# Two split orders and the doubled key columns in the last layer of a three-layer network

## The chip, the cores and the metric

One Trainium2 chip, one core of it. The metric is the device time of one execution in microseconds (us); lower is better. TensorE does the matrix products, VectorE and ScalarE the elementwise work, GpSimd and SyncE mostly start transfers.

## The reference, cut to what matters

The input is one sequence of 256 rows of 2048 columns in float32. Three layers follow each other: a convolution mixer with an MLP, a pooling mixer with an MLP, and a last layer with three kinds of attention. The change touches the last layer only, between its first products and its heads:

```python
h = rmsnorm_2(x, norm_g) @ w_in                    # 256 x 5388, split into 15 parts
c_q, c_kv, k_rope, ..., q_nsa, k_c, v_c, k_s, ...  # c_q, c_kv: 512 columns; k_c: 192; v_c: 128
q  = rmsnorm_2(c_q,  q_norm_g)  @ w_uq             # ranks -> 8 query heads
kv = rmsnorm_2(c_kv, kv_norm_g) @ w_ukv            # ranks -> 8 key and value heads
# compress: overlapping blocks of 32 rows, one every 16 rows (15 blocks)
k_cmp = silu((blocks(k_c) + pe_k).reshape(15, 32 * 192) @ w1k) @ w2k
v_cmp = silu((blocks(v_c) + pe_v).reshape(15, 32 * 128) @ w1v) @ w2v
```

The norm of `x` has one factor per row (r1). The kernel multiplies by it after the product, when it takes the result out of PSUM.

## The kernel before, in words

**Weights.** All weights run through one ring of four tiles (128 x 2048 numbers, 1 MB, smaller for some) in an order, the plan, that is fixed at build time. `Sync.load_tile` (line 950) starts the load of tile k into place k mod 4 when the products of tile k - 4 are done. Each float32 weight tile is split in two parts for the products: ScalarE writes the rounded part (`Act.split`, line 477, tile `hi`), and VectorE subtracts it from the tile and leaves the rest (`Dve.split`, line 590, tile `raw_r`, the "low" part). TensorE then does three products per block of 128 rows: high by high, high by low, low by high (lines 341). The compress weights `w_ck` and `w_cv` are used whole and are not split (`WHOLE`).

**The order of the work.** All engines run the same Python function `conduct`, and each keeps the instructions that are its own, so the order in which `conduct` calls things is the order of every engine's queue; waits are semaphores. `take(name)` hands out the next tile j and then calls `split_ahead(j + 3)`, which queues the splits of all tiles below that number whose load is already queued. `release(j, done, hold)` calls `load_ahead(j + 5)`, and unless `hold` is set it also calls `split_ahead(j + 4)`. So the split of tile j + 3 is queued when tile j is released, or, with `hold`, at the `take` of tile j + 1. Loads are queued by `release` in both cases.

**Small work between products.** `gemm` (line 1102) takes a tile, does its 24 products and calls `step()` in the middle of a tile and after its `release`. A step runs the next entry of the list `later`, and if that is empty the next of the list `extra`. `fill` runs an entry of `extra` alone.

**The stage around the change.** The products run in this order: `w_i2` (four tiles, 396 columns: k_rope, k_c, v_c and the gates), `w_i0` (four tiles, c_q), one compress piece of `w_ck`, `w_i1` (four tiles, c_kv, with a `w_ck` piece ahead of its last tile), then the heads: two tiles of `w_uq` with a `w_ck` piece between them, and so on. In the numbers of the plan: w_i2 is 332 to 335, w_i0 is 336 to 339, w_ck is 340, w_i1 is 341, 342, 343 and 345 with w_ck 344 between them, w_uq is 346 and 348 with w_ck 347 between, and 349.

- After `w_i2`, `evac` (line 1202) copies both 128-row halves from the PSUM banks to the staging tiles EV with the factor r1 (ScalarE, line 473). ScalarE makes the gates (tanh, line 540), VectorE finishes them, rotates the 64 k_rope columns of both halves (`rope`) and doubles them, and then `tail_rows` (VectorE, line 799) copies the last 64 of the 192 k_c columns twice, side by side, from EV to a tile of 128 columns for each half (`kc_t`, in R_s).
- `kc_turn` (line 1887) turns the first 128 k_c columns and these doubled 64 with four TensorE transposes (line 344). It is the second entry of `later`, so it stands in TensorE's queue right behind the products of tile 336.
- `ranked` (line 1830) is called for c_q (`w_i0`) and for c_kv (`w_i1`). After the products it takes the sum of squares of both halves out of PSUM (ScalarE, line 503), copies both halves to EV (ScalarE, line 473), computes the inverse root with VectorE and GpSimd (lines 582, 933, 574, 577) and multiplies EV by it (VectorE, line 582). The turns of the result are put into `later` behind three `fill` entries: the first two pairs stand behind the second tile of the next products.
- `compress_k` and `compress_v` (lines 1932 and 1942) each take one compress tile, do 8 or 16 small products and release it.

Of the kernel before, what the change touches and what calls it, by code (L numbers as in the profile page):

```python
# [153 lines left out]
def v3(ap, k):  # L154
    return ap.rearrange("p (k n) -> p k n", k=k)
# [142 lines left out]
class Engine:  # L298
# [26 lines left out]
    def idle(self, *a, **k):  # L325
# [7 lines left out]
        product = norm_mean = norm_root = relu_square = residual = rope = rope_keys = scale = scaled_parts = scores = side_load = side_taps = sine = \  # L333
# [233 lines left out]
        self.copy(xs, xs, done, scale=r)  # L567


class Dve(Engine):  # L570


# [218 lines left out]
    def group_sums(self, ready, done):  # L791

        self.wait_ge(ready)
        self.e.tensor_reduce(self.m.group_rows, self.m.group_of, AX.X, ALU.add).then_inc(*self.inc("dve_done", done))

    def tail_rows(self, t, src, ready, done):

        self.wait_ge(ready)
        self.cp(v3(self.m.kc_t[t], 2), src.unsqueeze(1).to_broadcast([128, 2, 64]), done)

    def tail_keys(self, b, ready, done):

# [176 lines left out]
def conduct(E, plan, listing):  # L979
# [3 lines left out]
    m, a, P, EV = E.m, E.a, E.m.P, E.m.EV  # L983
    serial = [0]

    def mark(what):
        serial[0] += 1
        return what, serial[0]
# [5 lines left out]
    def load_ahead(n):  # L994
        while at_["load"] < min(len(plan), n) and not listing:
            k = at_["load"]
            if k >= NS and k - NS not in freed:
                return
            name, i, parts, c = plan[k]
            E.load_tile(k, m.raw[k % NS][0:parts, 0:c], a[name][i], freed.get(k - NS))  # L1000
            at_["load"] += 1
# [36 lines left out]
    def release(j, done, hold=False):  # L1038
        freed[j] = done
        load_ahead(j + 1 + NS)  # L1040
        if not hold:
            split_ahead(j + 2 + AHEAD)


    bank_free, bank_held = [[] for _ in range(8)], set()
# [3 lines left out]
    def pair():  # L1049
        nxt["pair"] ^= 2  # L1050
        return [nxt["pair"], nxt["pair"] + 1]
# [41 lines left out]
    def flush():  # L1093
        while later:
            later.pop(0)()
# [6 lines left out]
    def gemm(name, xh, xl, x_names, nk, c, k0=0, steps=1, hold=False, lead=False, tail=False, late=False):  # L1102
        banks = pair()
        n = nk // 4
        groups = [[q] for q in range(n)]
        if lead:
            groups[0:2] = [[0, 1]]
        if tail:
            groups[-2:] = [[n - 2, n - 1]]
        done = [None, None]  # L1110

        def product(q, j, wh, wl, k, t):
            kk = k0 + 4 * q + k
            while x_names[kk] is None or (isinstance(x_names[kk], list) and x_names[kk][t] is None):
                step()
            x_ready = x_names[kk][t] if isinstance(x_names[kk], list) else x_names[kk]
            h, l = (x[kk][:, 128 * t:128 * t + 128] if isinstance(x, list) else x[:, kk, 128 * t:128 * t + 128] for x in (xh, xl))
            done[t] = ("product", j, t)
            E.product(P[banks[t]][:, 0:c], h, l, wh[:, k, :], wl[:, k, :], j, k, q == 0 and k == 0, q == n - 1 and k == 3,
                      x_ready, bank_free[banks[t]], done[t])  # L1120

        for group in groups:
            blocks = []
            for q in group:
                at_["pause"] = at_["pause"] or late and q == n - 1
                j, wh, wl = take(name)
                blocks.append((q, j, v3(wh, 4), v3(wl, 4)))
            turns = [(0, 1)] if len(group) == 1 else [(0,), (1,)]
            for ts in turns:
                for q, j, wh, wl in blocks:  # L1130
                    for k in range(4):
                        for t in ts:
                            product(q, j, wh, wl, k, t)
                        if k == 1 and steps > 1:
                            step(steps - 1)
                    if ts[-1] == 1:
                        release(j, done[1], hold and q == n - 1)
                    if steps:
                        step()
        return banks, done if tail else done[1]  # L1140
# [61 lines left out]
    def evac(banks, ready, c=512, scale=m.R1, scale_m=None):  # L1202
        ks, ms = [], []
        for t in range(2):
            k, done = ev(hold=True), mark("evacuated")
            E.copy_out(EV[k][:, 0:c], P[banks[t]][:, 0:c], [ready, scale_m], ev_free[k], done, scale=scale[:, t:t + 1])
            bank_free[banks[t]] = [done]
            ks.append(k)
            ms.append(done)
        return ks, ms  # L1210
# [12 lines left out]
    def side_load(sem, o, i, *free):  # L1223
        done = mark("side load")
        E.side_load(sem, o, i, list(free), done)
        return done
# [134 lines left out]
    XT, HH, HL, MH, ML, M, GA = m.XT, m.HH, m.HL, m.MH, m.ML, m.M, m.GA  # L1361
# [39 lines left out]
    h_m, r1_m, sq_m = [None] * 16, [], []  # L1401
# [188 lines left out]
    for n, kind in enumerate(kinds):  # L1590
        banks, done = gemm("w_z", HH, HL, h_m, 16, 512, steps=2)
# [3 lines left out]
        ks, ms = evac(banks, done, scale_m=list(r1_m))  # L1595
# [14 lines left out]
    for g in range(4):  # L1610
        banks, done = gemm("w_mo", MH, ML, mix_m, 16, 512, steps=3 if g == 0 else 1, hold=g == 3, tail=g == 3, late=g == 3)
# [141 lines left out]
    banks, done = gemm("w_mkv", HH, HL, memory["x"], 16, 512, steps=2, hold=True)  # L1753
    scale_m = load_row(2, 0, x_m[3])
    row_m = load_row(3, 1, x_m[3])
    ks, ms = evac(banks, done, scale=m.R4, scale_m=memory["r"])
# [18 lines left out]
    for c in range(0, 16, 2):  # L1775
        b, done = bank(), mark("windows")
# [6 lines left out]
    d_done = done  # L1783
# [7 lines left out]
    for g in range(4):  # L1791
        banks, done = gemm("w_p", MH, ML, d_m, 4, 512, k0=4 * g)
# [33 lines left out]
    h_m, r1_m, x_m = x_columns(x_get, HH, HL, GA[4])  # L1826
# [1 line left out]
    rope_m = side_load("c9", m.st[:, 32:160], a["c_rope"], memory["r"])  # L1828

    def ranked(name, th, tl, gain):  # L1830
        banks, done = gemm(name, HH, HL, h_m, 16, 512, steps=2)
        flush()
        sm = [square_sum(P[banks[t]][:, :], m.SUMC[:, t, :], [done, list(r1_m)], scale=m.R1[:, t:t + 1]) for t in range(2)]
        ks, ms = evac(banks, done, scale_m=list(r1_m))
        r = rstd(m.SUMC, 512, m.R3, sm)
        ns = [mark("ranked"), mark("ranked")]
        for t, k in enumerate(ks):
            E.scale(EV[k][:, :], EV[k][:, :], m.R3[:, t:t + 1], [r, ms[t]], ns[t])
        names, parts = columns(lambda t, c: EV[ks[t]][:, 128 * c:128 * c + 128], [ns], 4, th, tl, gain)

        def run(i):
            turned = both_of(parts[i])
            if i == 1:
                for k in ks:
                    let_go(k, turned)
        later.extend([fill, fill, fill, lambda: run(0), lambda: run(1)])
        return names
# [10 lines left out]
    banks, done = gemm("w_i2", HH, HL, h_m, 16, 396, steps=2, lead=True)  # L1858
    flush()
    ks, ms = evac(banks, done, 396, scale_m=list(r1_m))  # L1860
    side_load("c13", m.PEK, a["pe_k"], *x_m)
    side_load("c13", m.PEV, a["pe_v"])
    side_load("c13", m.C2K, a["w_c2k"])
# [12 lines left out]
    def kpe_turn():  # L1876
# [2 lines left out]
        E.rope_keys(b, done, list(gain_free), copied)  # L1879
        bank_free[b] = [copied]  # L1880
        kpe_m.extend([copied, done])

    kt = [mark("k tail"), mark("k tail")]
    for t in range(2):
        E.tail_rows(t, EV[ks[t]][:, 192:256], [ms[t], d_done], kt[t])

    def kc_turn():
        b, done, copied = bank(), mark("turn"), mark("copied")
# [43 lines left out]
    def compress_k(q):  # L1932
        if q == 0:
            cmp_m["b"] = bank(hold=True)
        b = cmp_m["b"]
        j, w = take("w_ck")
        rows = [8 * q + r for r in range(8)]
        E.compress(P[b][:, 0:192], [m.BK[:, l, :] for l in rows], [blk_m["a", q // 2] if q < 4 else blk_m["b", q - 4]] * 8,
                   v3(w, 8), q == 0, q == 5, j, bank_free[b], ("product", j, 1))
        release(j, ("product", j, 1))  # L1940

    def compress_v(q):
        b = cmp_m["b"]
        j, w = take("w_cv")
        rows = [16 * q + r for r in range(16)]
        E.compress(P[b][:, 192:320], [m.BV[:, l, :] for l in rows], [blk_m["v", l // 16] for l in rows],
                   v3(w, 16), q == 0, q == 1, j, None, ("product", j, 1))
        release(j, ("product", j, 1))
        cmp_m["done"] = ("product", j, 1)

    later += [nop, kc_turn, vc_turn, blocks_a, blocks_b, blocks_v, kpe_turn]
# [73 lines left out]
    banks, done = gemm("w_uq", m.CQH, m.CQL, cq_m, 4, 512, steps=2)  # L2025
# [15 lines left out]
    for g in range(2):  # L2041
        banks, ranks_done = gemm("w_ukv", m.CKH, m.CKL, ck_m, 4, 512, steps=2)
# [10 lines left out]
    banks, done = gemm("w_i3", HH, HL, h_m, 16, 512, steps=2)  # L2053
# [159 lines left out]
    banks, done = gemm("w_i4", HH, HL, h_m, 16, 512, steps=2)  # L2213
# [7 lines left out]
    banks, done = gemm("w_i5", HH, HL, h_m, 16, 384, steps=2)  # L2221
# [6 lines left out]
    banks, done = gemm("w_i6", HH, HL, h_m, 16, 512, steps=2)  # L2228
# [45 lines left out]
    for g in range(4):  # L2274
        banks, done = gemm("w_o2", oh, ol, o_cols, 16, 512, steps=2 if g == 0 else 1, tail=g == 3)
        for t in range(2):
# [4 lines left out]
            if g == 3:  # L2281
                r = rstd(m.SUMA, D, m.R2, [sums[2 * q + t] for q in range(4)], t)
# [87 lines left out]
```

## Time and profile before

| | us |
|---|---|
| median of three runs | 2367.03 |
| lowest and highest of them | 2365.26, 2368.86 |
| the profiled execution, its own time | 2365.16 |
| its span in the profile | 2363.4 |
| TensorE busy | 2336.7 (99%) |
| VectorE busy | 1303.4 (55%) |
| ScalarE busy | 1080.9 (46%) |

The span runs from the first to the last instruction; the other 1.8 us of the execution's time lie around it. TensorE is busy nearly all the time at a granted clock of 0.999 of full speed, so a change can win only what is left of its idle time, or lose by adding to it. The times at the start of rows below are counted from the start of the span.

### The profile page before, as it was taken

What the parts mean: (1) busy time and instruction counts of PE and PEld (TensorE: products, weight loads), DVE (VectorE), ACT (ScalarE), POOL (GpSimd) and SP (SyncE); (2) the same over time, 40 slices, a digit from 0 to 9 for tenths busy, and PEclk for the clock granted to TensorE, in tenths of its full rate; (3) what the DMA queues carried; (4) which work ended last, traced back from release to release, by engine and by line L of the source; (5) the groups of instructions that cost most, each with busy time, mean ns of one, the idle gap of its engine ahead of it and who ended that gap; (6) DMA issues with size and microseconds to landing.
All of it is one profiled execution on the core that took longest, in us unless ns stands there. A gap on an engine that the chain in (4) does not pass through costs nothing.

```text
span 2363.4 us, 25257 instructions
## 1 busy us (share of the span) xinstructions
PE 2336.7 (99%) x10937; PEld 1933.5 (82%) x10937; DVE 1303.4 (55%) x1325; ACT 1080.9 (46%) x1164; POOL 27.0 (1%) x46
## 2 busy tenths in 40 slices
PE   8999999999999999999999999999999999999998
PEld 6778788888888888888888888888888888888887
DVE  5665855544554554556764454554544584556654
ACT  6444444644344344354565444344344364344443
POOL 0000000000000000000000000000000010000000
PEclk9999999999999999999999999999999999999999
DMA  8445555555555555555555555555555545644444
GB/s 308 159 161 179 187 202 197 198 194 186 189 210 183 193 189 186 195 183 210 196 196 187 188 193 184 191 190 186 195 184 190 196 165 202 250 160 144 147 154 144
DMA packets 63871, 446.07 MB, mean 189 GB/s; under 512 B 7209, under 2 KB 7540, under 8 KB 12111
## 3 DMA queue, kind: packets, MB, share of 16 engines
q1 hardware_dynamic: 61280, 429.58, 51.4%
q0 software_dynamic: 2336, 14.76, 1.7%
q8 instruction: 86, 1.41, 0.2%
q10 hardware_dynamic: 144, 0.12, 0.0%
q14 instruction: 25, 0.20, 0.0%
HBM read 442.33 MB, written 2.10 MB: 188 GB/s over the span
## 4 chain that ended last, share of the span: by engine, by line
PE 95%; DVE 2%; ACT 1%; DMA 1%; issue 1%; POOL 0%; ACTq 0%; POOLq 0%; SPq 0%; DVEq 0%
PE P L341 92%; PE P L344 3%; DMA raw<-in_w_z 1%; ACT hi L477 1%; DVE raw_r L590 1%; DMA raw<-in_w_i 1%; ACT EV L473 0%; ACT EV L503 0%; DVE R_s L582 0%; DVE R_h L577 0%; ACT EV L557 0%; POOL st L933 0%; ACT EV L550 0%; ACT R_h L473 0%; DVE R_s L577 0%
## 5 line engine op out<-in xcount | busy, mean ns | idle before, releaser
L590 DVE TENSOR_TENSOR raw_r<-raw,hi 128x2048 fp32r<-128x2048 f32 (+3 forms) x411 | 911.3, 2219 | 960.6 <-ACT hi L477 959.6
L341 PE MATMUL P<-hi,R_h 128*128 128x512 f32 (+2 forms) x3840 | 1226.6, 394 | 10.0 <-DVE raw_r L590 8.9
L477 ACT ACTIVATE hi<-raw 128x2048 fp32r<-128x2048 f32 (+3 forms) x411 | 762.6, 1857 | 1018.1 <-DMA raw<-in_w_d 389.8
L341 PEld LDWEIGHTS P<-hi,R_h 128*128 128x128 f32 x3840 | 721.5, 188 | 161.3 <-issue 16.1
L341 PE MATMUL P<-hi,R_f_r 128*128 128x512 f32 x2480 | 777.4, 391 | 0.0
L341 PE MATMUL P<-raw_r,R_h 128*128 128x512 f32 (+2 forms) x1920 | 745.4, 388 | 0.0
L341 PEld LDWEIGHTS P<-hi,R_f_r 128*128 128x128 f32 x2480 | 465.6, 188 | 97.0 <-DVE raw_r L590 0.4
L341 PE MATMUL P<-raw_r,R_f_r 128*128 128x512 f32 x1240 | 482.7, 389 | 0.0
L341 PEld LDWEIGHTS P<-raw_r,R_h 128*128 128x128 f32 x1920 | 361.5, 188 | 73.3 <-issue 4.3
L341 PEld LDWEIGHTS P<-raw_r,R_f_r 128*128 128x128 f32 x1240 | 233.0, 188 | 47.1
L344 PE MATMUL P<-ident,EV 128*128 128x128 f32 (+1 forms) x476 | 71.4, 272 | 5.2 <-DVE R_s L585 2.8
L344 PEld LDWEIGHTS P<-ident,EV 128*128 128x128 f32 (+1 forms) x476 | 57.7, 139 | 19.9 <-issue 5.9
L574 DVE TENSOR_TENSOR R_m<-P,R_m 128x512 f32<-128x512 f32 x112 | 71.8, 681 | 0.1
L574 DVE TENSOR_TENSOR R_f_r<-P,R_f_r 128x512 fp32r<-128x512 f32 x66 | 45.0, 683 | 0.0
L533 ACT ACTIVATE EV<-P,st 128x512 f32<-128x512 f32 x64 | 42.9, 670 | 0.0
L535 ACT ACTIVATE EV<-EV 128x512 f32<-128x512 f32 x64 | 40.5, 633 | 2.0
L503 ACT ACTIVATE EV<-X 128x512 f32<-128x512 f32 x48 | 29.9, 633 | 23.3 <-DVE X L574 20.2
L473 ACT ACTIVATE R_f_r<-P 128x512 fp32r<-128x512 f32 x66 | 38.1, 579 | 1.7 <-PE P L344 1.7
L550 ACT ACTIVATE EV<-EV,STAT 128x256 f32<-128x256 f32 (+1 forms) x32 | 14.6, 456 | 51.7 <-DVE STAT L841 51.7
L503 ACT ACTIVATE EV<-R_m 128x512 f32<-128x512 f32 x24 | 15.0, 626 | 34.2 <-DVE R_m L574 34.2
L473 ACT ACTIVATE R_h<-P,cols 128x128 fp32r<-128x128 f32 (+1 forms) x64 | 21.4, 431 | 16.2 <-PE P L344 16.0
L341 PE MATMUL P<-R_f,R_s 65*128 65x512 f32 (+5 forms) x96 | 27.8, 418 | 0.0
(188 smaller groups left out, 763.0 us busy)
## 6 DMA issues: line engine op xcount, KB each, us to landing
raw<-in_w_u SPq DMA_DIRECT2D x128, 1024.0 KB, 4.8
raw<-in_w_d SPq DMA_DIRECT2D x128, 1024.0 KB, 4.8
raw<-in_w_z SPq DMA_DIRECT2D x47, 1024.0 KB, 4.9
raw<-in_w_i SPq DMA_DIRECT2D x36, 1024.0 KB, 4.8
raw<-in_w_mo SPq DMA_DIRECT2D x16, 1024.0 KB, 4.9
raw<-in_w_o SPq DMA_DIRECT2D x16, 1024.0 KB, 4.8
raw<-in_w_mkv SPq DMA_DIRECT2D x8, 1024.0 KB, 4.8
R_g<-in_rows POOLq DMA_DIRECT2D x6, 1024.0 KB, 5.3
```

Of the source, the lines that this page charges most:

```text
L341: return self.e.matmul(o, l, r, start=start, stop=stop, skip_group_check=True)
L344: return self.e.transpose(o, i, self.m.ident[0:i.shape[0], 0:i.shape[0]])
L473: self.e.activation(o, i, ACT.Copy, **scale).then_inc(*self.inc("act_done", done))
L477: self.e.activation(hi, raw, ACT.Copy).then_inc(*self.inc("high_made", ("high", k, d)))
L503: self.e.activation(dst, src, ACT.Square, accum_out=o, **scale).then_inc(*self.inc("act_done", done))
L533: self.e.activation(o, p, ACT.Relu, scale=r).then_inc(*self.inc("act_done", evacuated))
L535: self.e.activation(o, o, ACT.Square).then_inc(*self.inc("act_done", done))
L550: self.e.activation(E[:, o:o + n], E[:, o:o + n], ACT.Exp, bias=S[:, t:t + 1], accum_out=S[:, 2 + t:3 + t]).then_inc(*self.inc("act_done", ...
L574: self.e.tensor_tensor(o, a, b, op).then_inc(*self.inc("dve_done", *done))
L590: self.e.tensor_tensor(low, raw, hi.bitcast(f32), ALU.subtract).then_inc(*self.inc("low_made", *names))
```

## The change

`tail_rows` goes from VectorE to ScalarE: it reads the columns from the PSUM banks instead of EV, in two copies of 64 columns for each half instead of one of 128, with the factor r1, and is called right behind `evac`. The two banks are free after it. The products of `ranked` and the compress pieces release their (last) tile with `hold`, so that the next split is queued by the next `take`.

```diff
@@ class Act @@
+    def tail_rows(self, t, p, r, ready, done):
+        self.wait_ge(ready)
+        for d in range(2):
+            self.copy(self.m.kc_t[t][:, 64 * d:64 * d + 64], p, done, scale=r)
@@ class Dve @@
-    def tail_rows(self, t, src, ready, done):
-        self.wait_ge(ready)
-        self.cp(v3(self.m.kc_t[t], 2), src.unsqueeze(1).to_broadcast([128, 2, 64]), done)
@@ def ranked @@
-        banks, done = gemm(name, HH, HL, h_m, 16, 512, steps=2)
+        banks, done = gemm(name, HH, HL, h_m, 16, 512, steps=2, hold=True)
@@ behind w_i2 @@
     ks, ms = evac(banks, done, 396, scale_m=list(r1_m))
+    kt = [mark("k tail"), mark("k tail")]
+    for t in range(2):
+        E.tail_rows(t, P[banks[t]][:, 192:256], m.R1[:, t:t + 1], [ms[t], d_done], kt[t])
+        bank_free[banks[t]] = [kt[t]]
...
-    kt = [mark("k tail"), mark("k tail")]
-    for t in range(2):
-        E.tail_rows(t, EV[ks[t]][:, 192:256], [ms[t], d_done], kt[t])
@@ def compress_k, def compress_v @@
-        release(j, ("product", j, 1))
+        release(j, ("product", j, 1), True)
```

## Rows read from the trace of the kernel before

**Rows 1.** The page: busy time, share of the span, instructions.

```profile
PE 2336.7 (99%) x10937; PEld 1933.5 (82%) x10937; DVE 1303.4 (55%) x1325; ACT 1080.9 (46%) x1164; POOL 27.0 (1%) x46
```

**Rows 2.** Waits of PE, whole span: who waited for whom, total, times, longest.

```profile
PE P L341 <- DVE raw_r L590: 8.9, 2, 7.0
PE P L344 <- DVE R_s L585: 2.8, 1, 2.8
PE P L344 <- DVE EV L582: 1.4, 1, 1.4
```

**Rows 3.** Timeline of DVE, 1936 to 1947: start, length, work, idle before and releaser.

```profile
1936.86 4.49 DVE L590 TENSOR_TENSOR raw_r<-raw,hi 128x2048 fp32r<-128x2048 f32 x2
...
1943.91 0.35 DVE L585 COPY R_s<-EV 128x128 f32<-128x128 f32 x2
...
1944.34 2.28 DVE L590 TENSOR_TENSOR raw_r<-raw,hi 128x2048 fp32r<-128x2048 f32 x1
```

**Rows 4.** Timeline of PE, 1941 to 1996.

```profile
1944.41 0.41 PE L344 MATMUL P<-ident,EV 128*128 128x128 f32 x2 [2.83 <-DVE R_s L585]
...
1973.47 0.39 PE L341 MATMUL P<-hi,R_h 128*128 128x512 f32 x1
1975.22 0.63 PE L344 MATMUL P<-ident,EV 128*128 128x128 f32 x4 [1.36 <-DVE EV L582]
...
1987.92 0.39 PE L341 MATMUL P<-hi,R_h 128*128 128x512 f32 x1
...
1994.78 0.50 PE L341 MATMUL P<-R_f_r,hi 128*128 128x256 f32 x2
```

**Rows 5.** Timeline of ACT, 1936 to 1943.

```profile
1938.60 1.05 ACT L473 ACTIVATE EV<-P,st 128x396 f32<-128x396 f32 x2
1939.67 1.28 ACT L540 ACT_TABLE_LOAD   x1
1940.96 0.32 ACT L540 ACTIVATE R_g<-EV 128x12 f32<-128x12 f32 x2
1941.40 1.91 ACT L477 ACTIVATE hi<-raw 128x2048 fp32r<-128x2048 f32 x1
```

**Rows 6.** Groups of ACT by form, whole span: busy, mean ns, idle before.

```profile
L473 ACT ACTIVATE R_h<-P,cols 128x128 fp32r<-128x128 f32 x32 | 8.9, 384 | 11.8 <-PE P L344 11.8
...
L540 ACT ACTIVATE R_g<-EV 128x12 f32<-128x12 f32 x2 | 0.3, 206 | 0.0
```

**Rows 7.** Busy time of each engine in tile 336's products: stretch, sum, PE, PEld, ...

```profile
1936.19:1941.58 5.39, 5.38 (x24) 4.13 (x22) 5.15 (x9) 5.24 (x8) 4.66 (x8) 1.00 0.75 258
```

**Rows 8.** Chain that ended last, 1961 to 1976: start, length, what.

```profile
1961.95 6.47 DMA raw<-in_w_i
```

**Rows 9.** Timeline of ACT, 1960 to 1994.

```profile
1961.13 1.91 ACT L477 ACTIVATE hi<-raw 128x2048 fp32r<-128x2048 f32 x1 [3.64 <-DMA raw<-in_w_i]
1968.44 1.92 ACT L477 ACTIVATE hi<-raw 128x2048 fp32r<-128x2048 f32 x1 [5.40 <-DMA raw<-in_w_i]
1970.26 0.67 ACT L503 ACTIVATE EV<-P,st 128x512 f32<-128x512 f32 x1
...
1988.78 1.92 ACT L477 ACTIVATE hi<-raw 128x2048 fp32r<-128x2048 f32 x1 [7.06 <-DMA raw<-in_w_uq]
1990.60 0.67 ACT L503 ACTIVATE EV<-P,st 128x512 f32<-128x512 f32 x1
...
1993.06 0.61 ACT L473 ACTIVATE R_f<-P 128x512 f32<-128x512 f32 x1
```

**Rows 10.** Timeline of DVE, 1970 to 1996.

```profile
1970.39 2.29 DVE L590 TENSOR_TENSOR raw_r<-raw,hi 128x2048 fp32r<-128x2048 f32 x1 [5.02 <-ACT hi L477]
1972.60 0.16 DVE L582 TENSOR_SCALAR st<-st 128x2 f32<-128x2 f32 x1
...
1974.19 0.88 DVE L582 TENSOR_SCALAR EV<-EV,st 128x512 f32<-128x512 f32 x2
...
1990.73 2.29 DVE L590 TENSOR_TENSOR raw_r<-raw,hi 128x2048 fp32r<-128x2048 f32 x1 [6.68 <-ACT hi L477]
```

More of the change, by code:

```diff
@@ L1947, in compress_v @@
                    v3(w, 16), q == 0, q == 1, j, None, ("product", j, 1))
-        release(j, ("product", j, 1))
+        release(j, ("product", j, 1), True)
         cmp_m["done"] = ("product", j, 1)
```

## The prediction

> **What bounds the kernel now.** I read the first part of the profile page first: TensorE is busy for 2336.7 of 2363.4 us [rows 1], so all the rest of the span is 26.7 us, start and end included, and a change off TensorE can only win from that. Next its waits, by who released them [rows 2]: 8.9 us for the low parts of weights (two waits, the longer 7.0), 2.8 for a VectorE copy to R_s and 1.4 for a VectorE scaling of EV, each of the last two a single wait. The reader is to see that these two have the sizes of single places, and to find them in the timeline of TensorE [rows 4]. The first transpose of `kc_turn` starts at 1944.41 after 2.83 us of idling: TensorE was there at 1941.58. The first transpose of the c_q turn starts at 1975.22 after 1.36 us: it was there at 1973.86. Both are in the stage that the change edits. The question is therefore what ends each of these waits after the change, and whether the moved splits open another.
>
> **Wait A, the doubled key columns.** Before: ScalarE has both halves in EV at 38.60 + 1.05 = 1939.65 (I leave out the 19 where it is plain), but VectorE has two low splits in hand until 36.86 + 4.49 = 1941.35, then the gates and the rope work, and makes the two doubled copies only at 1943.91, 0.35 us for both [rows 3, 5]. TensorE resumes behind them. After: four ScalarE copies of 64 columns stand right behind `evac`. No row has such a copy. The nearest are one of 12 columns at 206 ns and one of 128 columns out of PSUM with a column as scale at 384 ns [rows 6]. Four of them cost 0.82 to 1.54 us, so the columns are ready between 1940.5 and 1941.2. I take 1.1 us, near the middle, as 64 lies between 12 and 128. TensorE needs them at 1941.58, so wait A goes completely at either end: a gain of 2.83 us, with 0.4 to 1.1 us to spare.
>
> The Trainium skill (ScalarE: Activation LUTs, section What ACT_TABLE_LOAD costs) gives 186 ns plus 0.833 ns a column, 93 ns more for a scale by pointer, and an overlap of 93 ns between neighbours. That would be 332 ns for one, an estimate from that page, and some 1.05 us for four. By it the sum is the same.
>
> What is late next there: the four copies push the tanh table load, the gates and the split of tile 339 (starting at 41.40) back by about 1.1 us [rows 5]. VectorE, free at 1941.35, waits about 1 us for the gates, and has 0.35 us less to do, so its next low split (tile 339, before from 44.34 to 46.62) ends at about 1947.3 [rows 3]. A tile of these products takes TensorE 5.39 us [rows 7]; from 1941.58 with two tiles between, tile 339 is wanted at about 1953. The cover is 5 us. The two low parts wanted first (337 and 338) are ready at 1941.35 at the latest, as before, and TensorE wants 338 only at about 1947.5. The copies of turned columns to R_s and the compress blocks queue on VectorE behind the low split and are wanted by the first compress piece at the end of `w_i0`, over 10 us later. The banks are freed about 1 us later; their next user is `w_i1`, 18 us on. GpSimd gets nothing new. From here on I write times as in the profile of before, without shifting them by 2.83.
>
> **Wait B, the split in front of the c_q sums.** This needs the order of calls. At the end of `w_i0` the last `step` runs the first compress piece (tile 340). `release(339)` queues the split of tile 342 and the release of 340 queued the split of 343, both ahead of the square sums. With `hold` at 339 the `take` of 340 still queues split 342 there; with `hold` at 340 split 343 moves behind sums, evacuation and scaling, to the `take` of 341. Its load starts only when `w_i0` is done, at 1961.95, and lands 6.47 us later [rows 8]: ScalarE stands for 5.40 us, splits at 1968.44, and only then takes the sums, at 1970.26 [rows 9]. VectorE follows: low part from 70.39, mean at 72.60, scaled columns at 74.19 + 0.88 = 1975.07 [rows 10]. After: ScalarE splits 342 (61.13 + 1.91 = 1963.04 [rows 9]), the sums can start there, 7.2 us earlier. VectorE's low part of 342, 2.29 us, lasts until about 1965.4; the mean, the root and the scaling, 2.47 us from 72.60 to 75.07 [rows 10], end at about 1968. TensorE wants them at 1973.86. Wait B goes, 1.36 us, with almost 6 to spare. Tile 343 itself is split when it lands, at 1968.44 as before, low part ready at 70.39 + 2.29 = 1972.7. TensorE wants it behind the four transposes, at about 1974.2: 1.5 us of cover. If the load landed 2 us later that cover would be gone and 0.5 us lost.
>
> **The new wait C, tile 348.** With `hold` at the end of `w_i1`, split 348 also moves behind the sums of c_kv. Before, ScalarE split it at 1988.78, when it landed, and VectorE had the low part at 90.73 + 2.29 = 1993.02; TensorE began with it at 1994.78, 1.76 us of cover [rows 4, 9, 10]. After: `w_i1` ends at 87.92 + 0.39 = 1988.31 [rows 4], and ScalarE goes at once to the sums. They and the evacuation took from 90.60 to 93.06 [rows 9], 2.46 us, so split 348 runs from about 1990.8 to 1992.7 and the low part to about 1995.05, 0.27 us after TensorE wants it. VectorE's norm chain (2.47 us from about 1989.8) ends at about 1992.3, just before the split is there. I take a loss of 0.3 us. Lower bound 0: the evacuation may start a little earlier or its tail overlap. Upper bound 0.8: if the chain of the norm starts only behind the whole evacuation, at 1990.8, it ends at 1993.3 and the low part at 1995.55. I take the value that the rows give.
>
> **The other edits, at nothing.** The other compress pieces stand at a `step` with the next `take` right behind and no work for ScalarE or VectorE between, or have no tile left to split at their release (the next one is whole, or not loaded). Their splits keep their place in both queues. `load_ahead` is called by `release` as before, so no transfer is moved in SyncE's queue, past nothing, and none is added. What hides it is that the order is the same; if I have missed a piece that costs a place in a queue, it costs up to one split, 1.9 us, where there is no cover. Behind the stage the last part of the plan follows in the same order.
>
> **Sum.** -2.83 - 1.36 + 0.3 = -3.9 us. The profiled execution took 2365.16 and would take 2361.3. It lies 1.87 below the median of the three runs, 2367.03, and the runs spread over 3.6 us; from the median the sum is 2363.1. As the median is what is compared, I forecast 2363, 0.17% below.
>
> **Rivals.**
> 1. No new wait. Where 348 is in time, both waits are won: -4.19, 2362.8. For it: C is only 0.27 by rows good to 0.1. Against: each of its terms is a measured length in an in-order queue.
> 2. The doubled columns stay late. Only the order in which table load and copies reach ScalarE decides: if the load (1.28 us [rows 5]) came ahead of the four copies, they end at 39.65 + 1.28 + 1.54 = 1942.5 at worst, 0.9 us after TensorE is there. The sum is then -3.0, 2364. Against it: the copies stand ahead of the tanh in program order, and copies ran before the load.
> 3. The change doesn't do what it says at B: if split 343 keeps a place ahead of the sums, by a call that I have read wrongly, B stays at 1.36 and the gain is 2.5, 2364.5. Against it: only `take` and `release` call for splits.
> 4. The other side: split 348's delay is handed on. TensorE is late at 348, but each later split waits on ScalarE for a transfer that starts when TensorE frees a place, so with compress tiles in the ring its cover could be less than a microsecond for each of the heads' tiles. It becomes slower than before when C and its followers together pass 4.2 us, and by over 0.2% when they pass 8.9: four late tiles at the longest form of C, 2.3 us (a whole split and a bit), would make 9.2 against 4.2, a time of 2372. For it: ScalarE idled for 7.06 us for one such transfer [rows 9], so the splits of this stage follow the transfers closely. Against: before, TensorE waited for a low part at two places only, 8.9 us in all, and for none here [rows 2, 4], and a late TensorE also wants the next tile later, so the delay does not add up.
>
> **How the numbers follow.** What a measurement of this kernel can tell from no change is about 0.2%, 4.7 us. Chances: the forecast 0.55, no new wait 0.17, the doubled columns late 0.1, B stays 0.08, handed on or another loss 0.1. The first two lie at 0.17 and 0.18%, under the bound by 0.5 to 0.8 us, which is less than the spread of the runs, so of their 0.72 I give 0.31 to faster by over 0.2%. Rivals 2 and 3 are within 0.2%. Of the last I give 0.07 to slower by over 0.2%. So faster 0.31, same 0.62, slower 0.07. The range: the sum's own bounds are -4.2 to -2.5 on either the median or the profiled execution, 2360.9 to 2364.5; with half of the spread of the runs on the upper side and a little on the lower, 2360.2 to 2366.3.
>
> **What would show it.** A: no idle time ahead of the transposes of `kc_turn`, four ScalarE copies from PSUM to R_s ahead of the table load, the last ending 0.4 us or more before TensorE arrives. B: the two square sums stand between the split of 342 and that of 343, the c_q transposes follow the products without a gap, and the low part of 343 is ready at least 1 us before its products. C: square sums at once behind `w_i1`, then split 348, and a wait of TensorE for `raw_r` of 0 to 0.8 us at the second tile of `w_uq`. Wrong would be: a wait for `raw_r` at 343, more than 1 us at 348, waits for `raw_r` further on, or a time outside the range while these three are as said, which would put the cause outside of this stage.

## The result and the profile after

| | before | after |
|---|---|---|
| median of 7 runs each, us | 2367.91 | 2361.0 |
| lowest and highest | 2365.26, 2370.84 | 2359.75, 2362.61 |
| profiled execution, its time and span | 2365.16, 2363.4 | 2361.19, 2359.4 |

The ratio is 0.9977, 95% interval 0.9968 to 0.9986: faster, by 3.3 to 7.6 us, 5.4 in the middle. The two medians in the table are 6.9 us apart, which is inside this interval; the argument below goes by the ratio. Whether the gain is more than 0.2% (4.7 us) the interval leaves open. The time of 2361.0 lies 2 us under the forecast of 2363 and inside the range of 2360.2 to 2366.3. In a second timing of the same kernel (below) the ratio was 0.9979 (0.9970 to 0.9987), 3.1 to 7.1 us. The spans of the two profiles differ by 4.0 us.

Waits of TensorE over the whole span, kernel after: who waited for whom, total, times, longest.

```profile
PE P L341 <- DVE raw_r L597: 9.6, 3, 7.5
PE P L344 <- ACT EV L473: 1.1, 3, 0.5
PE P L341 <- DVE R_h L584: 1.1, 2, 0.6
...
PE P L341 <- DVE R_m L592: 0.8, 1, 0.8
```

The last two lines of [rows 2], for R_s and EV, are gone. The waits for `raw_r` are three instead of two. Two of them, 7.5 and 1.8 us, stand at the start of the kernel, as two did before (7.0 and 1.9). The new one is in the timeline of TensorE, kernel after:

```profile
1941.47 0.39 PE L344 MATMUL P<-ident,EV 128*128 128x128 f32 x2
...
1970.72 0.60 PE L344 MATMUL P<-ident,EV 128*128 128x128 f32 x4
...
1990.60 0.50 PE L341 MATMUL P<-R_f_r,hi 128*128 128x256 f32 x2 [0.28 <-DVE raw_r L597]
```

Against [rows 4]: the key transposes start at 1941.47 with no idle time, those of c_q at 1970.72 with none, and the second tile of `w_uq` waits 0.28 us. The timeline of ScalarE, kernel after, shows what the order has become:

```profile
1938.57 1.06 ACT L473 ACTIVATE EV<-P,st 128x396 f32<-128x396 f32 x2
1939.51 0.94 ACT L473 ACTIVATE R_s<-P,st 128x64 f32<-128x64 f32 x4
1940.47 1.28 ACT L540 ACT_TABLE_LOAD   x1
...
1958.05 1.91 ACT L477 ACTIVATE hi<-raw 128x2048 fp32r<-128x2048 f32 x1 [3.48 <-DMA raw<-in_w_i]
1959.87 0.67 ACT L503 ACTIVATE EV<-P,st 128x512 f32<-128x512 f32 x1
...
1964.32 1.92 ACT L477 ACTIVATE hi<-raw 128x2048 fp32r<-128x2048 f32 x1 [1.87 <-DMA raw<-in_w_i]
...
1983.82 0.69 ACT L503 ACTIVATE EV<-P,st 128x512 f32<-128x512 f32 x1 [6.24 <-PE P L341]
...
1986.30 1.93 ACT L477 ACTIVATE hi<-raw 128x2048 fp32r<-128x2048 f32 x1
```

The four copies of 64 columns take 0.94 us and end at 1940.45, 1.0 us before TensorE comes. The c_q sums (1959.87) stand between split 342 (1958.05) and split 343 (1964.32). Compare [rows 9], where they stood behind the split of 343 and its 5.40 us of waiting. The scaled c_q columns are ready at 1964.68, 6.0 us before TensorE wants them. The low part of 343 is ready at 1968.57, 2.5 us before its products begin at 1971.08. The c_kv sums (1983.82) now stand ahead of split 348 (1986.30).

### The profile page after: what moved, and what is told of

The parts are those of the page before. It is cut to its first block, busy times and chain, and to the rows that moved or that the text cites. A ratio compares the mean times of both kernels' runs of the same rounds, so it can differ in the third digit from the quotient of the medians.

```text
span 2359.4 us, 25260 instructions
## 1 busy us (share of the span) xinstructions
PE 2336.0 (99%) x10937; PEld 1935.1 (82%) x10937; DVE 1304.0 (55%) x1323; ACT 1081.9 (46%) x1168; POOL 27.0 (1%) x46
## 4 chain that ended last, share of the span: by engine, by line
PE 95%; ACT 1%; DVE 1%; DMA 1%; issue 0%; ACTq 0%; POOLq 0%; POOL 0%; SPq 0%
PE P L341 93%; PE P L344 3%; DMA raw<-in_w_z 1%; ACT hi L477 1%; DVE raw_r L597 1%; ACT EV L473 0%; DMA raw<-in_w_i 0%; DVE R_s L589 0%; DVE R_h L584 0%; ACT EV L503 0%; ACT EV L557 0%; ACT EV L550 0%; DVE R_s L584 0%; DVE STAT L848 0%; DVE R_m L581 0%
```

## The experiments

Ratios are to the kernel before in runs on the same chip, with 95% intervals. Times in the spans can't be laid side by side directly: even without the wait there, TensorE reaches the key transposes anywhere between 1940.5 and 1942.8 us in the fourteen profiles. The four with the copies in their old place and the ten others both come there at 1941.4 on average. Waits can be laid side by side, and so can the stretch from the key transposes to the end, which is done below, with the late 348.

### The key columns alone

```diff
# changed kernel with the old releases
-        banks, done = gemm(name, HH, HL, h_m, 16, 512, steps=2, hold=True)
+        banks, done = gemm(name, HH, HL, h_m, 16, 512, steps=2)
-        release(j, ("product", j, 1), True)      # compress_k, compress_v
+        release(j, ("product", j, 1))
```

> Only the doubled key columns move to ScalarE; the splits keep their old order. Theory (two separate stalls, each with its own edit): no wait of TensorE at the key turn, the c_q wait back at about 1.4 us, no wait for raw_r at tile 348; span 2.8 us under the kernel before, with the start-up waits taken out. Rival (the two stalls are one, the second a consequence of the first): the c_q wait is gone as well, 4.2 us. Rival (the wait moves on): the 2.8 us show up again as longer waits later.

Ratio 0.9984 (0.9975 to 0.9993), 3.8 us in the middle. Timeline of TensorE, this kernel:

```profile
1940.96 0.38 PE L344 MATMUL P<-ident,EV 128*128 128x128 f32 x2
...
1971.65 0.63 PE L344 MATMUL P<-ident,EV 128*128 128x128 f32 x4 [1.28 <-DVE EV L589]
```

The key wait is gone, the c_q wait stays at 1.28 us and nothing waits at 348. The two stalls are separate.

### The holds alone

```diff
# kernel before, with
+        banks, done = gemm(name, HH, HL, h_m, 16, 512, steps=2, hold=True)
+        release(j, ("product", j, 1), True)      # compress_k, compress_v
```

> Only the holds; the doubled key columns stay with VectorE as before. Theory: the wait at the key turn stays at 2.8 us, the c_q wait is gone (1.36), and a wait of about 0.3 us for raw_r stands at tile 348: 1.1 us faster than before, which a timing can't tell from none. Rival (the stalls are one): the c_q wait stays, or tile 348 is in time because the stage runs later against the transfers.

Ratio 0.9997 (0.9988 to 1.0005), 0.7 us in the middle. The waits are as the theory has them. Timeline of TensorE, this kernel:

```profile
1944.90 0.66 PE L344 MATMUL P<-ident,EV 128*128 128x128 f32 x2 [2.83 <-DVE R_s L585]
...
1946.21 0.63 PE L341 MATMUL P<-raw_r,R_h 128*128 128x512 f32 x1
...
1949.53 0.38 PE L344 MATMUL P<-ident,EV 128*128 128x128 f32 x2
...
1995.45 0.50 PE L341 MATMUL P<-R_f_r,hi 128*128 128x256 f32 x2 [0.29 <-DVE raw_r L590]
```

But one thing is new. From the key transposes to the next turn, the same work, takes 49.53 - 44.90 = 4.63 us. In the first profile of the kernel before it took 47.62 - 44.41 [rows 4] = 3.21. A product of 512 columns behind the wait takes 0.63 us; the single ones in [rows 4] take 0.39. First the timeline of TensorE in the kernel before, then its busy time there (stretch, sum, TensorE, its weight loads, VectorE, ScalarE, GpSimd, granted clock, transfers), then the same for the holds-alone kernel:

```profile
1947.62 0.38 PE L344 MATMUL P<-ident,EV 128*128 128x128 f32 x2
```

```profile
1945.00:1947.00 2.00, 2.00 (x11) 1.63 (x10) 2.00 (x3) 0.00 (x0) 0.00 (x0) 1.00 0.06 25
```

```profile
1945.00:1947.00 2.00, 2.00 (x7) 1.77 (x8) 2.00 (x1) 0.00 (x0) 0.00 (x0) 0.50 0.26 108
```

The granted clock behind the wait is 1.00 (2.4 GHz) in the one and 0.50 (1.2 GHz) in the other, with the same 2.83 us of idle time ahead. The fall costs 4.63 - 3.21 = 1.42 us. The Trainium skill (TensorE: Matmul & The Clock Gate, section Part 1: The HAM clock gate) has this: a stretch without work lets the clock fall to half. The trace agrees in some executions and not in others.

### The kernel before, twice more

No edit.

> The kernel before once more, for its profile. Theory (the key wait of 2.8 us sometimes makes TensorE's granted clock fall, which costs about 1.4 us more behind it): the wait is 2.8 us again, and the clock behind it is either 1.00 as in the first profile or near 0.5 for some 2 us. If it is always 1.00 in this kernel, the fall in the holds-alone kernel is by itself and doesn't explain why the medians moved by 1 us more than the waits.

> A third look at the kernel before. The key wait is 2.83 us again; the clock behind it is at 0.5 for some 2 us if the fall is the usual case, as in two of three profiles with this wait so far, or 1.00 as in the first. The theory that the medians move by more than the waits because of it needs it to be common.

The key wait was 2.83 and 2.84 us. Busy time behind it, first of the earlier, then of the later of the two:

```profile
1943.00:1945.00 2.00, 1.27 (x5) 1.24 (x6) 1.97 (x6) 0.00 (x0) 0.00 (x0) 0.69 0.65 270
1945.00:1947.00 2.00, 2.00 (x6) 1.58 (x5) 1.97 (x4) 0.00 (x0) 0.00 (x0) 0.50 0.00 0
```

```profile
1945.00:1947.00 2.00, 2.00 (x11) 1.63 (x10) 1.97 (x4) 0.00 (x0) 0.00 (x0) 1.00 0.00 0
```

So the clock fell in one of three profiles of the kernel before, and in two of the four profiles that have this wait. What decides between the two no run here shows, and four profiles don't give the share. The two executions took 2366.75 and 2364.26 us. The c_q wait was 0.95 and 0.89 us here, not 1.36.

### Which hold does it

```diff
# e3b and e3c: the changed kernel without the rank hold
-        banks, done = gemm(name, HH, HL, h_m, 16, 512, steps=2, hold=True)
+        banks, done = gemm(name, HH, HL, h_m, 16, 512, steps=2)
# e4: the changed kernel without the compress holds
-        release(j, ("product", j, 1), True)
+        release(j, ("product", j, 1))
```

> The changed kernel without the hold on the rank products (compress holds and ScalarE tails stay). Theory: the hold at w_i0 does nothing, as the compress piece behind it queues the same split; the hold at w_i1 makes the late tile 348. So the c_q wait stays gone and the wait at 348, 0.28 us, goes too: 0.3 us faster than the changed kernel. Rival (the rank hold is what frees the c_q sums): the c_q wait is back at about 1.4 us, the kernel is 1.1 us slower than the changed one.

> The changed kernel without the hold on the compress pieces (the hold on the rank products and the ScalarE tails stay). Theory: the release of compress tile 340 again queues split 343 ahead of the c_q sums, so the c_q wait is back at 1.3 to 1.4 us, and tile 348 is still late by 0.3 us; span about 1.3 us over the changed kernel. Rival (the rank hold alone frees the sums): no c_q wait.

Without the rank hold there is no wait between the key turn and the heads at all: ratio 0.9975 (0.9966 to 0.9985). Without the compress holds the c_q wait is back and 348 is late as well: ratio 0.9984 (0.9974 to 0.9994). Timeline of TensorE, kernel with the rank hold only:

```profile
1971.34 0.63 PE L344 MATMUL P<-ident,EV 128*128 128x128 f32 x4 [0.59 <-DVE EV L589]
...
1991.21 0.50 PE L341 MATMUL P<-R_f_r,hi 128*128 128x256 f32 x2 [0.28 <-DVE raw_r L597]
```

So the compress holds win the c_q wait and the rank holds make the late tile. The two rank holds were only taken out together. That the one at `w_i1` makes 348 late and the one at `w_i0` does nothing is read from the order of the queue: 348 is the split that moved there. The size of the c_q wait I had wrong: 0.59 us instead of 1.3. The transfer of tile 343 shows why. Its rows in the chain that ended last, start and length: the kernel before in its second and third profile (waits 0.95 and 0.89), the kernel with the key columns alone (1.28) and this one (0.59):

```profile
1962.88 6.05 DMA raw<-in_w_i
1961.50 5.98 DMA raw<-in_w_i
1958.47 6.38 DMA raw<-in_w_i
1958.84 5.69 DMA raw<-in_w_i
```

With the first profile (6.47 us [rows 8], wait 1.36) these are five, and in each the wait is the length of the transfer less 5.1 us (5.09 to 5.11). The transfer's length differs between executions of one kernel, and the wait with it.

### The engine or the place in the queue

```diff
# e5: VectorE again, from EV, but called right behind evac
     ks, ms = evac(banks, done, 396, scale_m=list(r1_m))
+        E.tail_rows(t, EV[ks[t]][:, 192:256], [ms[t], d_done], kt[t])    # Dve.tail_rows as before
# e6: ScalarE, but behind the two gates
         E.gates(m.GATE[:, t, :], EV[ks[t]][:, 384:396], ms[t], list(gain_free), ga[t])
+    for t in range(2):
+        E.tail_rows(t, P[banks[t]][:, 192:256], m.R1[:, t:t + 1], [ms[t], d_done], kt[t])
```

> The changed kernel, but VectorE makes the doubled key columns as before (one copy of 128 a half, from EV), called right behind the evacuation instead of behind the rope work. Theory (the stall was the place in VectorE's queue, not the engine): VectorE is free at about 1941.4, needs 0.35 us, so the columns are there 0.2 to 0.4 us after TensorE; the key wait is 0.2 to 0.4 us instead of 2.8, and the time stands 0.3 us over the changed kernel. Rival (the engine matters): a wait of over 1 us stays.

> The changed kernel with the four ScalarE copies behind the gates, so behind the tanh table load (1.28 us) and the two gate instructions (0.32). Theory: the columns are ready 0.94 us after 1941.1 to 1941.3, at 1942.1 to 1942.2, and TensorE waits 0.5 to 0.7 us at the key turn, with its clock still at 1.00 behind it. Rival (the wait is not set by the columns): no wait. If the clock falls behind a wait this short, the price of the 2.8 us wait says nothing about its length.

VectorE, called right behind the evacuation, leaves 0.20 us of wait instead of 2.83, and its ratio, 0.9978 (0.9969 to 0.9987), is that of the changed kernel. ScalarE behind the table load and the gates leaves 0.82 us (0.5 to 0.7 was expected; its evacuation began 0.36 us later than in the changed kernel's profile, at 1938.93), and the clock behind it stays at 1.00. The place in the queue accounts for nearly all of the wait; between the engines, each in the early place, lie 0.20 us. Timeline of TensorE, the VectorE kernel and then the ScalarE one:

```profile
1941.66 0.41 PE L344 MATMUL P<-ident,EV 128*128 128x128 f32 x2 [0.20 <-DVE R_g L582]
```

```profile
1942.56 0.41 PE L344 MATMUL P<-ident,EV 128*128 128x128 f32 x2 [0.82 <-ACT R_s L473]
```

### Is a late 348 handed on

```diff
# e7: changed kernel, behind evac of w_i1: four more copies that repeat the evacuation
+            for n in range(4):
+                E.copy_out(EV[ks[n % 2]][:, 0:512], P[banks[n % 2]][:, 0:512], list(ms), None, again, scale=...)
```

> The changed kernel with four more evacuation copies of 512 columns on ScalarE between the c_kv evacuation and split 348 (they repeat what is there already). Theory (the wait at 348 grows one for one and is not handed on): the copies take 2.4 to 2.8 us, the wait at 348 is 2.7 to 3.1 us, no wait for raw_r follows it, and the span is 2.5 us longer; 1.4 us more if TensorE's clock falls in that wait as it did in the one at the key turn of the holds-alone kernel. Rival (delay handed on to the later heads' tiles): waits for raw_r at 349 to 356 as well, 5 us or more in all.

Ratio 1.0 (0.999 to 1.0009): 4.5 us over the changed kernel by the medians of two timings (2365.77 and 2361.28; the kernel before had 2366.05 and 2366.21 in them). Timeline of TensorE and busy time behind the wait, this kernel:

```profile
1993.06 0.51 PE L341 MATMUL P<-R_f_r,hi 128*128 128x256 f32 x2 [3.23 <-DVE raw_r L597]
```

```profile
1995.00:1997.00 2.00, 2.00 (x11) 2.00 (x11) 1.92 (x2) 0.82 (x1) 0.00 (x0) 0.50 0.04 15
```

The wait grew by 2.95 us to 3.23, a little over the 2.7 to 3.1 that were expected, and no wait for `raw_r` follows it. The delay isn't handed on. The clock is at 0.50 again behind the wait; with the price of the other fall the sum is 2.95 + 1.42 = 4.4. That most executions of this kernel had the fall is suggested by its median and not shown by one profile.

All profiles together test the price. Take the stretch from the first key transpose to the end of the span and subtract TensorE's waits in it. What is left is 414.7 to 415.1 us, 414.9 on average, in the eleven profiles without a fall, of kernels before and changed alike. In the three with one it is 416.3 (holds alone), 416.4 (this kernel) and 416.7 (kernel before, second profile): 1.4, 1.5 and 1.8 us more. So behind the key transposes the waits and the clock account for the time of each profile to some 0.3 us, and the change has no other price there.

One of those waits is outside the prediction. TensorE waits for R_m, small operands of the compress branch that VectorE copies, at about 2092 to 2097: 0.61, 1.74 and 0.68 us in the kernel before, 0.79 and 1.55 in the changed one, 0.35 to 1.66 in three of the others and not at all in the remaining six. It varies by more than wait B or C is worth.

### The changed kernel again, and one more edit

```diff
# e8: the changed kernel without the rank hold, and
-    extra += [cmp_last, nop, cmp_sums, nop, nop, cmp_turn, nop, cmp_out]
+    extra += [cmp_last, nop, cmp_sums, nop, cmp_turn, nop, nop, cmp_out]
```

> The changed kernel once more, on the same chip as the three others. Theory (three waits, sum -3.9 us): the ratio to before comes out near 0.9983, and the 6.9 us between the two medians of the first timing are mostly scatter of the runs. Rival (something outside the stage also gained some 2 to 3 us): the ratio stays near 0.997.

> The changed kernel without the hold on the rank products, and with cmp_turn one step earlier (the idle step behind it instead of ahead). Theory (the small copies behind cmp_turn wait in VectorE's queue behind a split whose transfer lands at varying times, which gives TensorE a wait of 0.6 to 1.7 us for R_m in five of the eight profiles): ahead of that split the copies are done before TensorE comes, the wait for R_m ahead of cmp_out is gone in any profile, and the kernel is 0.3 + about 1 us faster than the changed one. Rival (the earlier turn waits for the silu): a new wait ahead of the turn of the same size. Rival (no TensorE time is won, as another wait behind takes it).

> The kernel without the hold on the rank products once more, beside the best version on one chip. Theory: no wait between the key turn and the heads, clock 1.00 through the stage, median 1 us above the best version if the R_m wait is there. Rival: the two are the same.

The second timing of the changed kernel gave 0.9979, between the theory's 0.9983 and the rival's 0.997. In the kernel with the earlier turn (`cmp_turn` transposes the hidden values of the compress branch, and VectorE copies them to R_m) there is no wait for `R_m`: the small copies end at 2085.9, ahead of the split. In the changed kernel they stood behind it, at 2091.49. Timeline of VectorE in the new one:

```profile
2085.57 0.32 DVE L592 COPY R_m<-P 96x15 f32<-96x15 f32 x3
2088.86 2.29 DVE L597 TENSOR_TENSOR raw_r<-raw,hi 128x2048 fp32r<-128x2048 f32 x1 [2.97 <-ACT hi L477]
```

Its ratio is 0.9976 (0.9967 to 0.9985), median 2360.33. The kernel without the rank hold, on the same chip, had 0.9976 (0.9967 to 0.9986), median 2359.96, and in its profile of this timing had no wait for `R_m` either, though its small copies still stood behind the split. So the extra 1 us expected of the earlier turn is not there, and a wait behind it is longer (0.70 us at 2105.32, for EV, against 0.18 in that one). The timings don't tell the two apart, nor either from the changed kernel. That both beat the kernel before is shown. That they beat the changed kernel is not shown by the timings; for dropping the rank holds it is seen in the waits alone: 0.28 or 0.29 us at 348 in all six profiles of kernels with the rank hold (leaving out the one with four more copies), none in the four of changed kernels without it.

## Why the prediction was right, and where a size was off

- **Wait A.** Right in place, cause and length: 2.83 us gone. The copies cost 0.94 us where I took 1.1. The push on VectorE was hidden as said: its low split of 339 ended at 1947.08, where I took 1947.3.
- **The term that was mis-sized is A's price.** I took it as its 2.83 us of idle time. The profiles show that this idle time lets the clock fall in a part of the executions, for 1.4 to 1.8 us more. An estimate: with two falls in four profiles at 1.42 us that is 0.7 us on average. With B at its mean of 1.0 the sum becomes 2.8 + 0.7 + 1.0 - 0.3, some 4.3 us, against 5.4 and 5.0 in the two timings. The timings alone don't ask for it, as 3.9 lies inside both intervals too, and the last 0.7 to 1.1 us are not assigned to anything. The key columns alone are in line: 3.8 us by the ratio, but its interval (1.7 to 5.9) holds 2.83 as well as 3.5.
- **Wait B.** Right in cause, and in that the compress piece's release and not the one of `w_i0` counts. As a length, 1.36 was the longest of the five seen (1.36, 1.28, 0.95, 0.89, 0.59), so my term was about 0.3 us too large on average (1.01). It follows the landing of one transfer, which I had taken as fixed.
- **Wait C.** Predicted 0.3 us by 0.27 from rows, measured 0.28 or 0.29 in six profiles with the rank hold in place.
- **The edits at nothing.** The compress holds elsewhere opened no wait: C is the only new one behind the key transposes of the changed kernel, and the time outside of the waits is the same there. The wait for R_m varies with and without them.
- **The rivals.** No new wait: wrong, C is there. Table load first: not so here. Where it was made so, with the gates ahead of the copies as well, the wait was 0.82 us (up to 0.9 was said for the load alone, with slower copies). B stays: wrong. Handed on: wrong by the test that made the wait 3.2 us.
- **The 0.2% line.** I gave 0.62 to a gain within 0.2%. The measured middle is 0.23%, 0.7 us beyond that line, and the interval (0.14 to 0.32%) lies on both sides of it, so this isn't decided. The median after came 2 us under the forecast: the medians moved by 6.9 us where I had 3.9, while the median before, with four more runs, was 0.9 us higher. The falls of the clock explain a part of that and the spread of the runs (5.6 us before) may be the rest. That the number still lies in the range is owed in part to the width that I gave it for this spread.

## What to carry to other kernels

Price a stall of TensorE by its idle time plus what the clock may lose behind it, and look at the granted clock in more than one profile. The length of a wait in one profile is one draw where a transfer sets it. When a small operation is late, move its place in the queue before moving its engine. A split that waits for a transfer belongs behind the work that doesn't; but the same move costs where the next consumer is one short tile away, so each place is to be worked out by itself.

## What the runs showed of the hardware

- After idle times of TensorE of 2.83, 2.83, 2.83, 2.84 and 3.23 us in five profiles (before, holds alone, before again twice, late 348) its granted clock was 1.00, 0.50, 0.50, 1.00 and 0.50. A fall cost 1.4 to 1.8 us. After the waits of 1.36 us and less in this stage it was 1.00 each time, and so it was after the longest wait for R_m, 1.74 us.
- Four ScalarE copies of 64 columns out of PSUM with a column as scale took 0.94 us in a row, and 0.91 in the kernel where they stand behind the gates.
- The landing of one 1 MB tile, 343, varied without a change ahead of it: 6.47, 6.05 and 5.98 us in three profiles of the kernel before, 6.38 and 5.69 us in two of the others. A wait of TensorE that hung on it varied with it, from 1.36 to 0.59 us.
